# Decode values: page 0 scaled and the sum rounded on ScalarE, the rest made on VectorE, and the sum over tokens by rounded selector products

## The reference, cut to what matters

```
P = PAST_LEN                       # 256 = 2 pages of 128 tokens
a = diff_combine(s, lam, ...)      # softmax of logits 1 minus lam * softmax of logits 2, per head
return (einsum('bhqk,bkhv->bqhv', a[..., :P], v_past)
        + einsum('bhqk,bkhv->bqhv', a[..., P:], v_new))
```

## Time and profile before

| | |
|---|---|
| median of 3 runs | 2803.26 us (2803.26 to 2803.31) |
| profiled execution | 2801.9 us |
| its span in the trace | 2800.2 us |
| mean granted TensorE clock | 0.993 |
| TensorE busy | 2745.9 us, 98% |
| VectorE busy | 1192.6 us, 43% |
| GpSimd busy | 1098.9 us, 39% |
| ScalarE busy | 574.5 us, 21% |

### The profile page before, as it was taken

The page is one execution under the profiler, slowest core; times in us unless marked ns, Lnnn a source line. Parts: engine busy times, 40 slices in busy tenths (PEclk is TensorE's granted clock), DMA queues, the critical chain, the costliest instruction groups (busy, mean ns, idle before and its releaser), DMA issues.

```text
span 2800.2 us, 43463 instructions
## 1 busy us (share of the span) xinstructions
PE 2745.9 (98%) x17561; PEld 2666.8 (95%) x17561; DVE 1192.6 (43%) x2257; ACT 574.5 (21%) x1182; POOL 1098.9 (39%) x962
## 2 busy tenths in 40 slices
PE   7999999999999999999999999989999999999999
PEld 6999999999999999999999888877899999999999
DVE  4355544465333333333361334477433333333335
ACT  4222222223100000000030233364230000000003
POOL 4333333334444333333446324313533444443334
PEclk9999999999999999999999999999999999999999
DMA  3211111121111111111122111165211111111111
GB/s 107 61 54 55 55 54 55 47 100 47 46 46 46 51 55 47 46 46 46 46 93 68 56 44 52 40 219 202 84 46 46 46 46 46 46 46 47 55 50 62
DMA packets 202241, 175.06 MB, mean 63 GB/s; under 512 B 6290, under 2 KB 185093, under 8 KB 202062
## 3 DMA queue, kind: packets, MB, share of 16 engines
q1 hardware_dynamic: 162592, 141.67, 16.2%
q10 hardware_dynamic: 39470, 30.78, 3.4%
HBM read 147.06 MB, written 25.36 MB: 62 GB/s over the span
## 4 chain that ended last, share of the span: by engine, by line
PE 92%; DVE 4%; ACT 1%; POOL 1%; issue 1%; PEld 0%; DMA 0%; ACTq 0%; SPq 0%; DVEq 0%; POOLq 0%; PEldq 0%
PE ps L725 27%; PE ps L727 26%; PE ps L726 26%; PE ps L918 3%; PE ps L1178 2%; PE ps L1158 2%; POOL w_lo L681 1%; PE ps L904 1%; PE ps L951 1%; PE ps L960 1%; PE ps L1136 1%; PE ps L884 0%; PE ps L944 0%; PE ps L963 0%; POOL w_hi L677 0%
## 5 line engine op out<-in xcount | busy, mean ns | idle before, releaser
L725 PE MATMUL ps<-act_hi,w_hi 128*128 128x344 f32 (+2 forms) x3808 | 1242.3, 326 | 18.0 <-DVE act_lo L1935 7.7
L726 PE MATMUL ps<-act_lo,w_hi 128*128 128x344 f32 (+2 forms) x3808 | 1219.8, 320 | 0.0
L727 PE MATMUL ps<-act_hi,w_lo 128*128 128x344 f32 (+2 forms) x3808 | 1219.7, 320 | 0.0
L677 POOL TENSOR_TENSOR w_hi<-w_stage,ones 128x512 fp32r<-128x512 f32 (+1 forms) x412 | 426.8, 1067 | 1264.6 <-PEq L775 1095.0
L725 PEld LDWEIGHTS ps<-act_hi,w_hi 128*128 128x128 f32 x3808 | 718.3, 189 | 33.0 <-issue 23.8
L726 PEld LDWEIGHTS ps<-act_lo,w_hi 128*128 128x128 f32 x3808 | 718.2, 189 | 3.5 <-issue 1.7
L727 PEld LDWEIGHTS ps<-act_hi,w_lo 128*128 128x128 f32 x3808 | 718.0, 189 | 0.0
L681 POOL TENSOR_TENSOR w_lo<-w_stage,w_hi 128x512 fp32r<-128x512 f32 (+1 forms) x412 | 539.4, 1340 | 8.1
L725 PE MATMUL ps<-h_hi,w_hi 128*128 128x344 f32 x1056 | 339.3, 321 | 1.1 <-DVE resid L2144 1.1
L726 PE MATMUL ps<-h_lo,w_hi 128*128 128x344 f32 x1056 | 337.3, 319 | 0.0
L727 PE MATMUL ps<-h_hi,w_lo 128*128 128x344 f32 x1056 | 337.2, 319 | 0.0
(11 more groups left out here) (298 smaller groups left out, 2180.4 us busy)
## 6 DMA issues: line engine op xcount, KB each, us to landing
w_stage<-in_w_gate_up SPq DMA_DIRECT2D x88, 512.0 KB, 5.0
w_stage<-in_w_down SPq DMA_DIRECT2D x44, 512.0 KB, 4.1
w_stage<-in_w_in_a SPq DMA_DIRECT2D x32, 512.0 KB, 5.2
w_stage<-in_w_kv SPq DMA_DIRECT2D x16, 512.0 KB, 4.6
v_page<-in_cache_v SPq DMA_DIRECT2D x16, 512.0 KB, 7.6
w_stage<-in_w_out_b SPq DMA_DIRECT2D x12, 512.0 KB, 4.6
k_page<-in_cache_k SPq DMA_DIRECT2D x10, 512.0 KB, 4.9
x_spill<-resid ACTq DMA_DIRECT2D x8, 516.0 KB, 2.9
```

The costliest lines, as they stand in the source:

```text
L677: last = g.tensor_tensor(hi[:, part], WST[:, part], ones[:, 0:1].to_broadcast([P, quarter]), ALU.mult)
L725: pe.matmul(out, wh, xh, start=first, stop=False)
L726: pe.matmul(out, wh, xl, start=False, stop=False)
L727: return pe.matmul(out, wl, xh, start=False, stop=last)
```

## The change

ScalarE takes over the scaling of page 0 (`d_scale`, four instructions per request), and casts the finished sum to fp32r (`d_round`, one instruction of 128x1024) into the tile of page 1, which is no longer needed then. VectorE keeps the four instructions that add page 1 (`page_sum`), and gets one that subtracts the rounded sum from the sum (`page_rest`, 128x1024) into the tile of page 0, as fp32r. TensorE multiplies both parts by a selector in fp32r, `pick_rounded`: four fp32r products per request in place of two fp32 ones. Both streams are laid out one request ahead: ScalarE scales page b + 1 before it rounds sum b, and VectorE sums request b + 1 before it makes the rest of b. The semaphores `v_scaled` and `v_summed` are counted accordingly (`V_STEP`, `V_PART`). GpSimd makes the rounded selector once, among its constants at the start.

```diff
+        V_STEP = [1] + [2 * b for b in range(1, DEC)]
+        V_PART = [2 * b + 3 for b in range(DEC - 1)] + [2 * DEC]
...
+        VLO, VHI = ([at(f"v_page_{('lo', 'hi')[g]}{s}", [P, D], F32R, arena + 4096 * (2 * (s % 2) + g) + (16448 if s < 2 else 0))
+                     for s in range(4)] for g in range(NPG))
...
+            step(g.tensor_tensor(pickr[:], pick[:], ones[:, 0:16], ALU.mult))
...
             def d_value(b):
 
-                pe.wait_ge(v_summed, b + 1)
+                pe.wait_ge(v_summed, V_PART[b])
                 for u in range(2):
-                    last = pe.matmul(PS[0:DEC, 3 + u, :], pick[:, 7 - b:15 - b], VPG[b % 4][0][:, 512 * u:512 * (u + 1)],
-                                     start=(b == 0), stop=(b == DEC - 1))
+                    pe.matmul(PS[0:DEC, 3 + u, :], pickr[:, 7 - b:15 - b], VHI[b % 4][:, 512 * u:512 * (u + 1)],
+                              start=(b == 0), stop=False)
+                    last = pe.matmul(PS[0:DEC, 3 + u, :], pickr[:, 7 - b:15 - b], VLO[b % 4][:, 512 * u:512 * (u + 1)],
+                                     start=False, stop=(b == DEC - 1))
                 last.then_inc(pv_full, 1)
...
+            def d_scale(b):
+
+                act.wait_ge(v_page_in[b % 4], 32 * (b // 4 + 1))
+                act.wait_ge(d_dve, D_DVE["a"])
+                for h in range(AH):
+                    page = VPG[b % 4][0][:, 256 * h:256 * (h + 1)]
+                    last = a.activation(page, page, ACT.Copy, scale=DAS[:, 0, h * DEC + b:h * DEC + b + 1])
+                last.then_inc(v_scaled, 1)
+
+            def d_round(b):
+
+                act.wait_ge(v_summed, V_STEP[b])
+                a.copy(VHI[b % 4][:], VPG[b % 4][0][:]).then_inc(v_scaled, 1)
...
+            d_scale(0)
             act.wait_ge(at_o, AH * NB + OPENED)
             for c in (6, 7):
                 a.copy(XH[:, c, EARLY_ROWS * P:SEQ], QA[:, c, EARLY_ROWS * P:SEQ]).then_inc(late_hi, 1)
-            for s in range(2):
-                act.wait_ge(new_turned, s + 1)
-                a.copy(RWS[s][:].rearrange("p (u n) -> p u n", u=2), PS[0:DEC, 5:7, :]).then_inc(new_rows, 1)
-            x_reload(6)
-            x_reload(7)
+            for b in range(DEC):
+                if b + 1 < DEC:
+                    d_scale(b + 1)
+                d_round(b)
+                if b == 0:
+                    new_rows_copy(0)
+                elif b == 1:
+                    x_reload(6)
+                    x_reload(7)
+                elif b == 2:
+                    new_rows_copy(1)
...
-            def page_values(b):
+            def page_sum(b):
...
-                for h in range(AH):
-                    part = slice(256 * h, 256 * (h + 1))
-                    last = v.tensor_scalar(slot[0][:, part], slot[0][:, part], DAS[:, 0, h * DEC + b:h * DEC + b + 1], None, ALU.mult)
-                last.then_inc(v_scaled, 1)
-                dve.wait_ge(v_scaled, b + 1)
+                dve.wait_ge(v_scaled, V_STEP[b])
...
+            def page_rest(b):
+
+                dve.wait_ge(v_scaled, V_PART[b])
+                v.tensor_tensor(VLO[b % 4][:], VPG[b % 4][0][:], VHI[b % 4][:], ALU.subtract).then_inc(v_summed, 1)
...
+            page_sum(0)
             for b in range(DEC):
-                page_values(b)
+                if b + 1 < DEC:
+                    page_sum(b + 1)
+                page_rest(b)
                 wob_add(b + 2)
```

More of the change, by code:

```diff
@@ L114, in build @@
         pick = place("pick", [P, 16])
+        pickr = place("pick_rounded", [P, 16], F32R)
         CT = place("vectors", [P, 80])
@@ L1847, in _, with new_rows_copy @@
             a.copy(DAN[:], PS[:, 6, 0:64]).then_inc(d_act, 1)
+            def d_scale(b):
[8 more added lines that the diff above has]
+                a.copy(VHI[b % 4][:], VPG[b % 4][0][:]).then_inc(v_scaled, 1)
+            def new_rows_copy(s):
+                act.wait_ge(new_turned, s + 1)
+                a.copy(RWS[s][:].rearrange("p (u n) -> p u n", u=2), PS[0:DEC, 5:7, :]).then_inc(new_rows, 1)
+            d_scale(0)
             act.wait_ge(at_o, AH * NB + OPENED)
```

## The result

The changed kernel takes **2811.11 us** (median of 13 executions, 2808.37 to 2813.95), the kernel before 2803.26 (13 executions beside it, 2801.4 to 2805.57): a ratio of 1.0028, 95% interval 1.0019 to 1.0036, or 7.85 us more. It is slower by a little more than the 0.2% named in the prediction. The forecast was 2808.5, its range 2801.0 to 2813.0.

What follows compares the result with a forecast made beforehand. TensorE, busy 98% of the span, was taken as the bound. Group 7 9.3 us late, then 22.6 us instead of 26.49 to group 11, gave +5.4, rounded to +5.2: 2803.26 + 5.2 = 2808.5 us, range 2801.0 to 2813.0.

Steps and rivals of the forecast that it cites:

- A value saves 1.0 us: On TensorE, four fp32r products taken as 0.95 us replace 1.92 us per value; 8.0 us over eight values.
- Durations: Per request: scale 1.6 us and round 1.0 on ScalarE, sum 1.68 and rest 1.2 on VectorE.
- Value 0 waits 3.1: TensorE waits 3.1 us at value 0 for VectorE's rest 0, behind sum 1; group 4 starts 2.2 us late.
- A fall of the clock after value 0: TensorE's clock drops to 0.50 after value 0's wait, costing 1.6 us and delaying GpSimd's release by 0.4.
- The split takes 11.4: GpSimd's split of slab S_WOB+2, stretched by VectorE's instructions beside it, takes 11.4 us and ends at 1951.0, against 1946.80.
- the rival of the full lock: Short VectorE instructions shut GpSimd out in full too: split 13.6 us, +7.4 in all, 2810.7; chance 0.10.
- Page 4 lands 8.05 after the split: Request 4's page lands 8.05 us after GpSimd's split instead of 10.55, since two residual reloads leave its way.
- the rival of the late page: Page 4 lands no earlier than now, 10.55 us after the split; value 3 2.5 later, +7.7, 2811.0; chance 0.18.
- Value 3 behind sum 4 and scale 4: Rest 3 and round 3 queue behind work awaiting page 4; TensorE waits some 8.5 us, group 7 9.3 late.
- Groups 7 to 11, 3.9 us shorter: TensorE from group 7's start to group 11's: 22.6 us against 26.49, with shorter values, two waits gone, one clock fall.
- Nothing at value 6: Rest 6 is done by about 1980, value 6 wants it at about 1980.5; it just fits, no wait counted.
- The full gain: Rounding runs far enough ahead that value 3 doesn't wait: -9.5 us, 2793.8; chance 0.06.

Runs made afterwards that it cites:

- e2: Changed kernel with SyncE's loads of pages 4 to 6 issued ahead of weight slab S_WOB+3: 2799.19 us, ratio 0.9989 to the kernel before.
- e4: Changed kernel with ScalarE's two reloads of the residual put behind the second copy of new rows: 2811.46 us, ratio 1.0026 to the kernel before.
- e5: Changed kernel with page_rest as four instructions of 128x256 in place of one of 128x1024: 2812.23 us, one execution.
- e9: As e2, with round and rest of page 6 also ahead of page 7's scale and sum: 2798.49 us, ratio 0.9982 to the kernel before.
- e1: Changed kernel with round and rest of requests 3 to 6 ahead of the next page's scale and sum: 2807.64 us, ratio 1.0017 to the kernel before.
- e7: As e2, with every value laid one group later on TensorE: 2802.5 us, ratio 0.9997 to the kernel before.
- e6: As e2, with round and rest of requests 0 and 1 ahead of the next scale and sum: 2804.16 us, ratio 1.0004 to the kernel before.
- e8: As e7, with round and rest of pages 1 and 6 ahead of the next page's scale and sum: 2800.6 us, ratio 0.9993 to the kernel before.

## Why the prediction came out as it did

Step by step, in the prediction's order:

- **A value saves 1.0 us: right.** 0.93 us at the upper clock for the 0.95 taken; a slow step out didn't stay. From one value to the next TensorE takes 5.13 us without waits, 6.21 before: 1.08 less, since the lead-in of 0.09 that the prediction rounded for went too.
- **Durations: right.** Scale 1.70 (1.6 taken), sum 1.68, round 1.03 (1.0), rest 1.22 (1.2).
- **Value 0 waits 3.1: right** (3.02). Group 4 starts 4.99 us into the stretch, where it was 2.78 before: 2.2 late, as said.
- **A fall of the clock after value 0: not in this execution.** It stayed at 1.00, as in e2, e4, e5 and e9, but fell in e1 after the same wait of 3.02 us, and cost group 4 1.56 us there, for the 1.6 taken. So the size was right and the certainty wrong. The 0.4 us that the fall was to add to GpSimd's release fell away (1.25 us from group 4's start, where 1.36 + 0.4 was taken).
- **The split takes 11.4: too little**, it took 12.2. The two halves lost 2.0 and 1.05 us against the split that runs alone; 1.5 of the 2.0 fell on GpSimd's first instruction, which took 2.52 us beside the end of sum 2 and rest 1. The prediction's estimate from the rule of the Trainium skill (SBUF — State Buffer, Who interferes with whom), full exclusion, was 13.6; this trace lies nearer to the forecast (0.8 above it) than to the rule (1.4 below), so the rival of the full lock didn't come. e5 shows that cutting the long instruction up doesn't free the split (11.9).
- **Page 4 lands 8.05 after the split: mis-sized**, 8.8. That is beyond the 8.5 from which the rival of the late page was to decide, though of its extra 2.5 us only 0.8 came. The reason given for the earlier landing, the reloads, is not shown (e4).
- **Landing to value 3, 4.55: right**, 4.7.
- **Value 3 behind sum 4 and scale 4: right** in kind and place, shown by e1 and e2. The wait is 11.5 instead of 8.5; TensorE, with its clock up, also came to it 1.7 us earlier than forecast. What counts is group 7's start: 9.3 us late was forecast, 11.3 came (22.3 us into the stretch before, 33.7 now). The 2.0 between are the split (+0.8), the page (+0.8), the low clock in value 3 itself (+0.75), which the sum had counted behind it alone, landing to value 3 (+0.1), and the release (-0.5).
- **Groups 7 to 11, 3.9 us shorter: nearly right**, 4.6 (26.49 before, 21.9 now). The lead-ins gave 0.3 more, and of the low clock 1.4 us fell here (group 7 takes 5.57 us instead of 4.20). With the 0.75 in value 3 this fall cost 2.1 us, where 1.6 was taken.
- **Nothing at value 6: right.** It found its operand at 1985.45 without a wait; rest 6 had ended 1.0 us before.

The sum by these measured terms is +11.3 - 4.6 = +6.7, which agrees with the 6.6 of the stretch; forecast were +5.4, rounded to +5.2. The mechanism was right. Split and page were each 0.8 us too small and the fall of the clock 0.5; the release without the first fall (0.5) and the lead-ins (0.3) gave some of it back. Of the 2.6 us between forecast and median 1.4 come from the stretch and 1.2 from outside it. The result crossed the 0.2% line, to which the forecast gave 0.43, against 0.51 for a time within it: the side that it held likelier was not the one that came. The upper bound was also added a little short (late page and full lock, 4.7 above 2808.5, make 2813.2, not 2813.0), which changes nothing here. The full gain, the rival of 0.06, was out of reach in this order of loads. But e9 got 5 us of it (0.18%, 0.09 to 0.27) with the loads moved and one rest brought forward.

## What to carry to other kernels

A pipeline laid one step ahead makes each step wait for the next one's data: before it is written, look for the step whose input arrives late, and put what is already computable ahead of that wait. A change that shortens the bounding engine by microseconds can be more than undone by a load that stood late but harmless in a queue (11.4 us against 8), so the queue's order belongs to the change. And where a second engine slows a neighbour by contention, moving one wait hands the delay to whatever stands behind the slowed instruction; follow it through all customers, the PSUM adds too.

## What the runs showed of the hardware

- The granted clock did not follow the length of a wait alone. It stayed at 1.00 after 3.02 us (changed kernel, value 0), 3.03 (e2), 3.01 (e7, value 1) and 3.22 (e5, value 0), but fell to 0.50 after 3.02 us in e1 (value 0, behind the same instructions as in the changed kernel), after 3.03 in e6 (value 2), after 2.71 in e8 and after 1.98 in e7 (value 6). What tells these apart was not settled. In e7 (window, us, TensorE busy, granted clock, DMA share, GB/s), around a wait that kept the clock and one that lost it:

```profile
1948.00:1950.00 2.00, 0.00 (x0) 1.00 0.58 236
1950.00:1952.00 2.00, 1.81 (x10) 1.00 0.01 2
...
1976.00:1978.00 2.00, 0.02 (x2) 1.00 0.01 4
1978.00:1980.00 2.00, 2.00 (x8) 0.77 0.96 301
1980.00:1982.00 2.00, 2.00 (x8) 0.50 0.64 220
```

- ScalarE's scaling takes 1.70 to 1.72 us beside GpSimd's split and without it, while VectorE's sums of four instructions, where all four stand beside it, go from 1.67 to between 4.2 and 5.8 us, and a rest from 1.22 to 2.31.
- Cutting a subtraction into four spared GpSimd 0.3 us of a split and cost VectorE 3.4 us (5.72 instead of 2.31): each of the four quarters took as long as one instruction of GpSimd beside it (1.43 us instead of 0.36, GpSimd's 1.39).
